# Blocks of a matmul's moving operand at a stride of 1536 in place of 1408 bytes, all at multiples of 256

## What is computed

```python
for i in range(2):
    y = short_conv_mixer(x, ...) if i == 0 else pool_mixer(x, ...)
    h = layer_norm(ALPHA * x + y, ln1_g[i], ln1_b[i])
    r = jax.nn.relu(h @ mlp_w1[i])                 # 1024 -> 4096
    f = (r * r) @ mlp_w2[i]                        # 4096 -> 1024
    e = (p[i] @ ple_w[i]) * jax.nn.sigmoid(h @ ple_gate_w[i])   # p: 256 token inputs
    x = layer_norm(ALPHA * h + f + e, ln2_g[i], ln2_b[i])
```

## Time and profile before

| | |
|---|---|
| median of 3 runs | 2122.08 us (2120.86 to 2122.61) |
| profiled execution, its own time | 2117.3 us |
| its span, first to last instruction | 2115.5 us |
| tensor engine busy | 2104.1 us, 99% |
| vector engine busy | 1266.2 us, 60% |
| scalar engine busy | 822.8 us, 39% |
| granted clock of the tensor engine | 0.999 |

### The profile page before, as it was taken

One profiled execution on the slowest core, in us unless ns is written; L12 is line 12 of the kernel. 1 busy time (PEld: TensorE's weight loads), 2 busy tenths in 40 slices (PEclk: granted clock), 3 DMA queues, 4 the chain that ended last, 5 costly groups with the idle time before them and its releaser, 6 DMA issues.

```text
span 2115.5 us, 31857 instructions
## 1 busy us (share of the span) xinstructions
PE 2104.1 (99%) x13221; PEld 2100.6 (99%) x13221; DVE 1266.2 (60%) x1892; ACT 822.8 (39%) x1288; POOL 73.5 (3%) x67
## 2 busy tenths in 40 slices
PE   9999999999999999999999999999999999999998
PEld 9999999999999999999999999999999999999998
DVE  5233367786454444444777877888875346645478
ACT  4222233653433222222543645555443324233345
POOL 0000000000000000000020002000300000000000
PEclk9999999999999999999999999999999999999999
DMA  4010231443222111111112344543222212122233
GB/s 174 30 59 30 69 130 47 132 143 121 67 93 87 51 50 41 43 58 41 60 60 81 103 134 130 169 137 121 62 77 92 68 51 68 53 80 80 65 105 133
DMA packets 53777, 179.68 MB, mean 85 GB/s; under 512 B 8080, under 2 KB 10512, under 8 KB 53648
## 3 DMA queue, kind: packets, MB, share of 16 engines
q1 hardware_dynamic: 50768, 177.33, 25.5%
q10 hardware_dynamic: 2880, 0.52, 0.2%
HBM read 173.36 MB, written 4.46 MB: 84 GB/s over the span
## 4 chain that ended last, share of the span: by engine, by line
PE 98%; DVE 1%; ACT 1%; DMA 0%; SPq 0%; issue 0%; DVEq 0%; ACTq 0%
PE ps L697 33%; PE ps L698 32%; PE ps L699 32%; ACT acc L955 0%; DMA x_raw<-x_t 0%; DVE acc L1173 0%; PE ps L749 0%; PE ps L750 0%; DVE std L1213 0%; PE ps L726 0%; PE ps L732 0%; ACT w_split L880 0%; SPq L641 0%; PE ps L781 0%; DVE acc L1297 0%
## 5 line engine op out<-in xcount | busy, mean ns | idle before, releaser
L697 PE MATMUL ps<-h_hi,w_split 128*128 128x352 f32 x2160 | 697.8, 323 | 1.6 <-ACT t L1005 0.7
L698 PE MATMUL ps<-h_lo,w_split 128*128 128x352 f32 x2160 | 692.5, 321 | 0.0
L699 PE MATMUL ps<-h_hi,w_split 128*128 128x352 f32 x2160 | 692.3, 321 | 0.0
L697 PE MATMUL ps<-r_hi,w_split 128*128 128x352 f32 x1634 | 527.3, 323 | 0.0
L698 PE MATMUL ps<-r_lo,w_split 128*128 128x352 f32 x1634 | 523.7, 320 | 0.0
L699 PE MATMUL ps<-r_hi,w_split 128*128 128x352 f32 x1634 | 523.5, 320 | 0.0
L1297 DVE TENSOR_TENSOR acc<-acc,ps 128x352 f32<-128x352 f32 (+1 forms) x769 | 374.2, 518 | 133.5 <-PE ps L699 132.8
L616 DVE TENSOR_TENSOR w_split<-w_raw,w_split 128x1024 fp32r<-128x1024 f32 x291 | 357.8, 1251 | 111.3 <-ACT w_split L880 110.6
L697 PEld LDWEIGHTS ps<-h_hi,w_split 128*128 128x128 f32 x2160 | 405.6, 188 | 3.3 <-issue 2.0
L698 PEld LDWEIGHTS ps<-h_lo,w_split 128*128 128x128 f32 x2160 | 406.4, 188 | 0.0
L699 PEld LDWEIGHTS ps<-h_hi,w_split 128*128 128x128 f32 x2160 | 405.1, 188 | 0.0
(11 more groups left out here) (128 smaller groups left out, 1191.8 us busy)
## 6 DMA issues: line engine op xcount, KB each, us to landing
w_raw<-w_stream SPq DMA_DIRECT2D x315, 512.0 KB, 3.5
x_raw<-x_t SPq DMA_DIRECT2D x4, 704.0 KB, 8.2
y_t<-acc SPq DMA_DIRECT2D x4, 704.0 KB, 4.0
w_raw<-p_t SPq DMA_DIRECT2D x6, 352.0 KB, 2.9
y_t<-acc SPq DMA_DIRECT2D x3, 352.0 KB, 2.2
w_raw<-w_stream SPq DMA_DIRECT2D x3, 256.0 KB, 5.0
x_raw<-x_t SPq DMA_DIRECT2D x4, 176.0 KB, 4.2
x_raw<-x_t SPq DMA_DIRECT2D x2, 352.0 KB, 5.9
```

Source lines behind the costliest of these rows:

```text
L697: pe.matmul(out, wh, mov_h, start=first, stop=False)
L698: pe.matmul(out, wh, mov_l, start=False, stop=False)
L699: return pe.matmul(out, wl, mov_h, start=False, stop=last)
```

## The change

r_hi and r_lo become tensors of R_BLOCKS = 6 blocks with a stride of R_STRIDE = 384 elements (1536 bytes), of which the first 352 are used. r_hi starts at the last multiple of 256 bytes that leaves room behind it for r_lo, t and y_scaled_t inside x_lo: 9600 bytes into x_lo, where it was 11,264. r_lo follows 9216 bytes on, again at a multiple of 256; t and y_scaled_t follow r_lo. The splits of the token inputs write two blocks of 352 at that stride from 704 elements in a row. Nothing else is different; the blocks of x and h stay as they are.

```diff
-        rh, at = place("r_hi", [P, NG * CHUNK * TG], F32R, at3)
-        rl, at = place("r_lo", [P, NG * CHUNK * TG], F32R, at)
+        R_BLOCKS, R_STRIDE = NG * CHUNK, -(-TG * 4 // 256) * 64
+        at_r = (end2 - 2 * R_BLOCKS * R_STRIDE * 4 - 4 * TG * 4) // 256 * 256
+        assert at_r >= at2 + 3 * 2 * WIN * 4
+        r_hi, at = place("r_hi", [P, R_BLOCKS, R_STRIDE], F32R, at_r)
+        r_lo, at = place("r_lo", [P, R_BLOCKS, R_STRIDE], F32R, at)
+        rh, rl = r_hi[:, :, 0:TG], r_lo[:, :, 0:TG]
...
         def rpart(t, n, f):
-            at = (n * CHUNK + f) * TG
-            return t[:, at:at + TG]
+            return t[:, n * CHUNK + f, :]
+
+        def rparts(t, n):
+
+            return t[:, n * CHUNK:(n + 1) * CHUNK, :]
+
+        def token_inputs(u):
+            return raw[:, u.q, 0:KP * TG].rearrange("p (k t) -> p k t", k=KP)
...
-                cols = slice(slot[1] * KP * TG, (slot[1] + 1) * KP * TG)
-                ins = eng.tensor_tensor(rl[:, cols], raw[:, u.q, 0:KP * TG], f32(rh[:, cols]), ALU.subtract)
+                ins = eng.tensor_tensor(rparts(rl, slot[1]), token_inputs(u), f32(rparts(rh, slot[1])), ALU.subtract)
...
-                    n = slot[1]
-                    act.copy(rh[:, n * KP * TG:(n + 1) * KP * TG], raw[:, u.q, 0:KP * TG]).then_inc(w_hi, 1)
+                    act.copy(rparts(rh, slot[1]), token_inputs(u)).then_inc(w_hi, 1)
```

## The result

The changed kernel takes 2155.0 us (median of 5, 2153.06 to 2156.45) against 2122.08 us. The ratio is 1.015, with a 95% interval of 1.0139 to 1.016: slower by 33 us, where 2.9 us less were forecast.

A forecast was written before the change was run, and what follows sets the result against it. The tensor engine, never idle, was taken as the bound: matmul count times start interval. 4902 r matmuls saving 0.6 ns each gave 2.9 us, all else 0, so 2122.1 - 2.9 = 2119.2 us; range 2114.8 to 2123.6.

The forecast's parts named there:

- What bounds the kernel: Whole kernel: tensor engine busy 2104.1 of 2115.5 us, so time is number of matmuls times the interval between starts.
- Price (a): All r matmuls at multiples of 256 gain 0.6 ns each: 4902 x 0.6 ns = 2.9 us.
- block 1: Opening, conv_in(0): nine matmuls in a row at a multiple of 256, 158.9 ns each, taken as the aligned pace.
- The range: Whole time: 2114.8 us, just under each moved matmul saving 2.8 ns, to 2123.6, no change plus run spread.
- uniform alignment is worse: Rival on r's stream: one alignment collides with itself, 321.2 to 323.3 ns, 10.3 us slower, 2132.4 us; chance 0.07.
- block 2: Opening, conv_in(0): nine matmuls in a row at 128 past a multiple of 256, 161.1 ns each, records of 323.3 ns.
- No effect: Rival on r's matmuls: the opening's difference is not alignment, or the saving is lost: 2122.1 us; chance 0.16.
- Writers and placement: Scalar and vector engine splits cost at most 2.1 us, covered, so 0 on the path; moving r and t: 0.

The follow-up runs named there:

- norm0: Changed kernel with the layer-norm sums moved from blocks 4 and 6 of h's tensors to 5 and 7, at multiples of 256: 2119.74 us beside 2121.77.
- norm3: Changed kernel with the first of each two norm matmuls issued twice, so three at 128 past: 2120.54 us, 0.9991 against the kernel before.
- norm3_pair128: norm3 plus one extra pair of matmuls, once, ahead of a down step, reading a block at 128 past a multiple of 256: 2138.88 us (1.009).
- norm3_pair0: norm3 plus one extra pair of matmuls, once, ahead of a down step, reading a block at a multiple of 256: 2122.58 us (1.0014).
- u128: Changed kernel with all r blocks at 128 past a multiple of 256, stride 1536 kept: 2124.68 us beside 2120.14 (1.002).
- u64: Changed kernel with all r blocks at 64 past a multiple of 256, stride 1536 kept: 2128.5 us beside 2121.77 (1.0033).
- alt0: Changed kernel with r's stride back at 1408 and its base left at a multiple of 256, so blocks alternate: 2119.7 us beside 2120.14 (0.9999).
- pair0: norm0 plus one extra pair of matmuls, once, ahead of a down step, reading block 5, at a multiple of 256: 2131.79 us.
- before_norm0: Kernel before with norm0's edit of the norm sums and nothing else: 2128.45 us (1.0036).

## Why the prediction was wrong

**What bounds the kernel.** Right, and still so: the tensor engine has no idle time to speak of, no wait was added, and the time is the number of matmuls times the interval.

**Price (a), 0.6 ns for a matmul at multiples of 256.** Right for one of two paces. Where the changed stream runs fast it takes 158.3 ns, and 48 r matmuls take 7.60 us, the figure that the prediction gave. norm0 and norm3 run mostly so, and before has 158.9: the 0.6 ns are there. None of it shows in the time, since norm0 and norm3 are no faster than before beyond their intervals.

**The step that failed** is the sentence "All at a multiple should look like block 1". It took the interval for a function of the alignment of a matmul, so that a short stretch would show what a long one does. The runs show that it depends on what ran before as well: the same instructions at the same addresses run at 158.3 or 166.7 ns for hundreds of microseconds, and two matmuls decide which (norm3_pair128 against norm3_pair0: 2138.88 and 2122.58 us). The changed kernel paid 325.9 ns a record on r, where the sum had 320.6. The nine matmuls of the opening's block 1 were a sample of something near the fast pace. Nothing in the trace of before could show the slow one, since no stream there stays at one alignment for more than nine matmuls. What it did show, and was not weighed, is that L697 has 323 ns and L698 and L699 have 320 and 321 in the earlier trace rows, though each line reads the two alignments half and half: a possible sign that the neighbours count (in norm0, with all r blocks alike, the three lines are at 321).

**The range.** It rested on the opening's stretches as bounds and so had no term for a pace that lasts. The rival "uniform alignment is worse" named the right side and a collision of the uniform stream with itself, but took its size from block 2 (10.3 us, at 0.07), where the slow pace has 7 ns on a record in place of 2.1 and takes h along. And it is not uniformity alone: u128 and u64 cost 4.5 and 6.7 us.

**"No effect", and the page on the tensor engine's clock.** The fixed surplus that the Trainium skill states in "TensorE: Matmul & The Clock Gate", section "Wait — 56ns, not 53.3ns?", did not hold here, with float32r operands and a weight load for every matmul: at 352 columns and full clock the surplus over 146.7 ns was 11.6 ns at the one pace and 20.0 at the other, neither 2.5 nor fixed.

**Writers and placement.** At nothing, rightly: the scalar engine's busy time went from 822.8 to 822.9 us and the vector engine's from 1266.2 to 1271.0. Of these 4.8 us, 4.6 are on the addition to acc (374.2 to 378.8 us), which the change doesn't touch; the six splits keep their 781 and 892 ns, so writing at a stride cost nothing that shows. None of the rise is on the path, and alt0 shows that the place costs nothing.

**What stays open.** What in the chip makes the slow pace: no run looks inside. The runs tie it to moving blocks that all start at a multiple of 256 and to what ran just ahead; the slices of w_split stayed at 128 past in all of them, so their part in it wasn't tried. Nor is it known why two matmuls at 128 past change the pace and three don't, or what makes a stall enter or leave it: two h matmuls 0.43 us apart stand where the slow pace ends in norm3_pair128, at 1202 us, and at 1206 us in pair0, where it goes on.

## What to carry to other kernels

When an engine is never idle and its instructions have a surplus that depends on the operands' place, a layout must be judged by long streams in the real order, with the rare instructions between them; a stretch of nine tells the price of one pace. After such a change compare the count of instructions in equal stretches of a few hundred microseconds: two levels where one was are a lasting pace of its own, and what stands at the step is the first suspect for its trigger, to be tested by moving it. A layout that alternates may be worth keeping, not because it is the fastest, but because its paces lie closer together here: 158.9 and 160.0 ns, which cost before_norm0 7 us, where 158.3 and 166.7 cost the changed kernel 33.

## What the runs showed of the hardware that was not expected

Streams of 352-column matmuls, never idle, at the full 2.4 GHz clock, have several steady paces: on r at multiples of 256, 158.3 and 166.7 ns from start to start; with r_lo 128 past, 160.0; alternating, 158.9 and 160.0. The changed kernel's two executions had 160.0 and 158.9 ns in the same conv stage. A pair of matmuls of 0.3 us, or a stall, moves the stream from one pace to another, in either direction, and then it holds for hundreds of microseconds: 570 us in the changed kernel, 924 us in pair0.
